# Three places of a two-block kernel: the first tiles, the head of the first feed-forward, and the last norm

## The chip, the cores and the metric

The kernel runs on one core of one Trainium2 chip. The metric is the device time of one execution in microseconds (us). Several executions of the kernel before were timed, and one more was profiled; times inside a profile count from the start of its span.

## The reference

Two transformer blocks follow each other on one sequence of 256 tokens with 1024 channels, in fp32. The first has a mixer of three parts (an RWKV-7 recurrence, a sparse attention, a state-space scan), a gated convolutional feed-forward of width 2816, and a gate by a second input. The second has a pooling layer and a dilated attention layer, each with its own feed-forward, and ends in a norm:

```python
def _rmsnorm(x, g):              # as rms_norm of the first block
    return x * lax.rsqrt(jnp.mean(x * x, axis=-1, keepdims=True) + eps) * g
...
h = _modulate(_rmsnorm(x, norm2_g[layer]), sh2, sc2)     # x_norm * (1 + sc2) + sh2
x = x + g2[:, None, :] * _conv_ffn(h, ffn_w_up[layer], ffn_conv_w[layer], ffn_conv_b[layer], ffn_w_down[layer])
...
return _rmsnorm(x, final_g)
```

The changed places compute: the first two tiles of `z = rms_norm(x, pre_mix_norm) @ w_in`; the start of `gelu(gate) * up`, where gate and up are the two halves of a causal depthwise convolution (three taps and a bias) of `x @ w_up`; the vectors `(1 + scale) * gain` of four later norms; and the last norm.

## The kernel before, in words

Activations lie transposed: channels on the 128 partitions in eight groups (`KT` = 8, index `k`), tokens along the free axis (`T` = 256). `h` is the residual. Each product is made in three passes of a reduced-precision fp32 format: an operand is split into a high part and a low part (the operand less its high part), and a tile sums high by high, high by low and low by high over the eight `k`, 24 products of 128x128 weights with 256 columns. A feed-forward's down tile sums over 22 channel groups, 66 products.

Weights are read in order through a ring of six slots of 1 MB (`ring`), issued by SP, which waits until the chunk six before is used. ScalarE writes a chunk's high part (`ring_hi`, four slots; `early_hi` for the first twelve chunks, which are those of the first projection), and GpSimd the low part in place (`ring_lo`); for the first twelve chunks VectorE does that, but GpSimd for the very first one (semaphore `first_lo`, L1483). On ScalarE the high parts stand between its other work: `reach(job)`, called before it reads the bank of `job`, makes all high parts whose slots depend on TensorE work older than that job; `take` calls it, `take0` does not. A second argument limits how many are made at a call.

TensorE opens a bank of PSUM for every job, in a rotation over eight banks; `opened` waits until the bank's previous job is given back by its reader. `close` counts finished jobs in `psum_ready`.

A norm: squares of `h` on ScalarE, six of them summed by VectorE, the sums over channels on TensorE against a column of 1/1024 (`mean_square_of`, job `("ms", i)`), square root on ScalarE (`root(i)`), reciprocal on VectorE into two columns of `rs` (tokens on the partitions, one column for each half of the tokens), and `spread(i)` on TensorE, which copies the two columns along all partitions by a product with the identity (job `("wd", i)`). VectorE then scales `h`.

The start: x is transposed in, normed with the squares taken over tokens' rows, and for each `k` VectorE scales, ScalarE writes the high part (`x_high`, 128x256 `hn_hi`), VectorE the low part (`x_split`, `hn_lo`). TensorE runs `first_tiles`: for each `k` two products with the high part of the activation (weights high and low) for both tiles, then all products with the low part. The parameter transposes (`("par", 0)`, `("par", 1)`) come behind them.

The first feed-forward (`ffn(0)`) works on pairs of tiles: gate ("ug") j and j+1, up ("uu") j and j+1. Its norm is divided out behind the product: for each tile VectorE multiplies by the spread root `wide_sb` (`normed`), ScalarE makes the last tap with the bias (`own`, into `ct`), VectorE adds the other two taps (`convolved`, 128x255 each), ScalarE takes GELU of the gate (`gated`), VectorE multiplies (`product`) and splits (`act_low`). The second tap of an up tile gives its bank back. VectorE's `second_gains` runs behind the first pair: four `(scale + 1) * gain` of 128x8 into `gsc`. They are used from the second block's first norm on, and GpSimd waits for them before it makes mask constants between its low parts.

The end: behind the last feed-forward's eight down tiles (`ffn(2)`), norm 9 runs as above, VectorE writes `h * final * wide` into `hn` for eight `k`, TensorE transposes sixteen 128x128 pieces into four banks (`("fin", n)`), VectorE copies two of them out and ScalarE two, and SP sends each half row block (128x512, 256 KB) to the output (L1440).

Line numbers: L549 is every product, L559 a transpose of `turn`, L1291 a transpose of attention, L2393 every ScalarE activation, L1646, L1653 and L1656 are VectorE's tensor-tensor, scalar-tensor-tensor and copy, L1579 a low part on GpSimd, L1483 that of the first chunk, L1531 and L1537 operations of GpSimd's sine tables.

## Time and profile before

| | us |
|---|---|
| runs of the kernel before | 1360.19, 1361.86, 1362.41 (median 1361.86) |
| the profiled execution | 1360.57 |
| its span | 1358.1 |
| TensorE busy in it | 1286.5 (95%) |
| VectorE, ScalarE, GpSimd busy | 571.7, 618.4, 845.2 |
| mean granted TensorE clock | 0.965 of full speed |

The span is the stretch between the first and the last instruction; the execution's own time is longer by what lies around it. Busy times of engines overlap each other. TensorE's products are pipelined: one may be listed as 0.28 us long while the next starts 0.12 us behind it.

### The profile page before, as it was taken

The page shows a single profiled execution, that of the slowest core. Times are in us where ns is not written, and L with a number is a line of the kernel's source. Part 1 is how long each engine was busy: PE and PEld are TensorE (multiplying, and loading weights), DVE is VectorE, ACT ScalarE, POOL GpSimd, SP SyncE. Part 2 cuts the span into 40 slices and gives each one's busy share as a digit, 9 for nine tenths or more (in the row PEclk, how much of TensorE's full clock was granted, in tenths as well). Part 3 has the DMA queues.
Part 4 walks back from the last instruction along what each step waited for, and adds up shares of the span by engine and source line. Part 5 has one row for each costly group of instructions (what it writes and reads, how often), then busy time and mean ns, then how long its engine had stood idle before and what let it go on. Part 6 is the DMA issues. An engine that isn't in the chain of part 4 may idle for free.

```text
span 1358.1 us, 25788 instructions
## 1 busy us (share of the span) xinstructions
PE 1286.5 (95%) x10741; PEld 1199.3 (88%) x10741; DVE 571.7 (42%) x1287; ACT 618.4 (46%) x953; POOL 845.2 (62%) x433
## 2 busy tenths in 40 slices
PE   6997989889899999898999999999999998999998
PEld 5983447779799999898999999999998888999997
DVE  5658676642676671522433303122222224433302
ACT  4540443125565554654544434554534454544431
POOL 7985400026689888555688776846655665888781
PEclk9998979989999999899999998999999999999998
DMA  8759985603455555425455555453648793455440
GB/s 265 199 168 361 328 293 189 216 31 113 136 187 186 175 176 182 152 94 187 141 180 180 167 193 165 140 156 93 188 127 256 240 294 122 155 179 182 165 162 31
DMA packets 232816, 242.81 MB, mean 179 GB/s; under 512 B 9068, under 2 KB 201726, under 8 KB 232702
## 3 DMA queue, kind: packets, MB, share of 16 engines
q1 hardware_dynamic: 232382, 241.08, 54.5%
q8 instruction: 85, 1.39, 0.4%
q14 instruction: 29, 0.24, 0.1%
q10 hardware_dynamic: 320, 0.10, 0.0%
HBM read 240.11 MB, written 1.05 MB: 178 GB/s over the span
## 4 chain that ended last, share of the span: by engine, by line
PE 90%; DVE 5%; ACT 2%; issue 2%; POOL 0%; ACTq 0%; DVEq 0%
PE banks L549 88%; DVE arena L1646 1%; PE banks L1291 1%; DVE arena L1653 1%; PE banks L559 1%; ACT ring_hi L2393 1%; ACT arena L2393 0%; DVE banks L1653 0%; DVE banks L1646 0%; POOL ring_lo L1483 0%; ACTq L1401 0%; PE banks L846 0%; ACT hn_hi L2393 0%; ACT hn L2393 0%; DVE hn L1653 0%
## 5 line engine op out<-in xcount | busy, mean ns | idle before, releaser
L1579 POOL TENSOR_TENSOR ring_lo<-ring,ring_hi 128x2048 fp32r<-128x2048 f32 (+1 forms) x176 | 718.8, 4095 | 437.0 <-ACT ring_hi L2393 436.8
L549 PE MATMUL banks<-hn_hi,ring_lo 128*128 128x256 f32 (+1 forms) x1864 | 528.8, 287 | 0.0
L549 PE MATMUL banks<-hn_hi,ring_hi 128*128 128x256 f32 x1696 | 484.0, 289 | 14.4 <-ACT hn_hi L2393 11.0
L549 PE MATMUL banks<-hn_lo,ring_hi 128*128 128x256 f32 x1696 | 446.4, 283 | 0.0
L2393 ACT ACTIVATE ring_hi<-ring 128x2048 fp32r<-128x2048 f32 (+1 forms) x176 | 299.6, 1705 | 172.1 <-PE banks L549 128.1
L549 PEld LDWEIGHTS banks<-hn_hi,ring_lo 128*128 128x128 f32 (+1 forms) x1864 | 366.0, 196 | 0.1
L549 PEld LDWEIGHTS banks<-hn_hi,ring_hi 128*128 128x128 f32 x1696 | 333.1, 196 | 18.0 <-issue 9.6
L549 PEld LDWEIGHTS banks<-hn_lo,ring_hi 128*128 128x128 f32 x1696 | 311.2, 192 | 0.1
L2393 ACT ACTIVATE arena<-banks 128x256 f32<-128x256 f32 (+6 forms) x240 | 94.0, 411 | 257.8 <-PE banks L549 176.4
L549 PEld LDWEIGHTS banks<-arena 64*128 64x128 f32 (+4 forms) x1282 | 118.9, 182 | 66.3 <-issue 42.6
L549 PE MATMUL banks<-arena 128*64 128x128 f32 (+9 forms) x1282 | 147.3, 309 | 24.4 <-DVE arena L1646 9.8
L549 PE MATMUL banks<-act_hi,ring_hi 128*128 128x256 f32 x528 | 149.6, 283 | 0.0
L549 PE MATMUL banks<-act_hi,ring_lo 128*128 128x256 f32 x528 | 149.4, 283 | 0.0
L549 PE MATMUL banks<-act_lo,ring_hi 128*128 128x256 f32 x528 | 149.4, 283 | 0.0
L1653 DVE SCALAR_TENSOR_TENSOR arena<-banks,par,arena 128x255 f32<-128x255 f32 (+1 forms) x187 | 89.6, 481 | 124.4 <-ACT arena L2393 122.0
L2393 ACT ACTIVATE arena<-banks,par 128x256 f32<-128x256 f32 x88 | 49.6, 564 | 122.6 <-PE banks L549 69.3
L549 PEld LDWEIGHTS banks<-act_lo,ring_hi 128*128 128x128 f32 x528 | 101.4, 192 | 0.0
L549 PEld LDWEIGHTS banks<-act_hi,ring_hi 128*128 128x128 f32 x528 | 101.4, 192 | 0.0
L549 PEld LDWEIGHTS banks<-act_hi,ring_lo 128*128 128x128 f32 x528 | 101.4, 192 | 0.0
L1653 DVE SCALAR_TENSOR_TENSOR h<-banks,mod,h 128x256 f32<-128x256 f32 x32 | 15.5, 484 | 133.7 <-PE banks L549 133.7
L2393 ACT ACTIVATE arena<-arena 128x256 f32<-128x256 f32 (+4 forms) x97 | 46.8, 511 | 39.7 <-DVE arena L1646 13.4
L549 PE MATMUL banks<-ring_lo,hn_hi 128*128 128x256 f32 x208 | 58.9, 283 | 0.0
(259 smaller groups left out, 1586.5 us busy)
## 6 DMA issues: line engine op xcount, KB each, us to landing
ring<-in_ada_w_dram SPq DMA_DIRECT2D x48, 1024.0 KB, 8.5
ring<-in_ffn_w_up_dram SPq DMA_DIRECT2D x44, 1024.0 KB, 5.2
ring<-in_w_up_dram SPq DMA_DIRECT2D x22, 1024.0 KB, 5.1
ring<-in_ffn_w_down_dram SPq DMA_DIRECT2D x16, 1024.0 KB, 5.0
ring<-in_w_kv_dram SPq DMA_DIRECT2D x15, 1024.0 KB, 5.4
ring<-in_w_in_dram SPq DMA_DIRECT2D x9, 1024.0 KB, 8.6
ring<-in_w_kv_dram SPq DMA_DIRECT2D x18, 512.0 KB, 3.8
ring<-in_attn_w_q_dram SPq DMA_DIRECT2D x18, 512.0 KB, 3.9
```

The lines of the kernel that those rows point to most:

```text
L549: return nc.tensor.matmul(o, l, r, start=start, stop=stop, **k)
L559: last = nc.tensor.transpose(b[0:m, off:off + n], src, ident[0:n, 0:n])
L1291: last = nc.tensor.transpose(b[:, br * P:br * P + P], dsc[s][:, x, k * P:k * P + P], ident[:, :])
L1579: led.emit(g.tensor_tensor(low, raw, high.bitcast(F32), ALU.subtract), sem("lo_ready"))
L1646: led.emit(v.tensor_tensor(o, x, y, op), signal, value)
L1653: led.emit(v.scalar_tensor_tensor(out=o, in0=x, scalar=s, in1=y, op0=op0, op1=op1), signal, value)
L2393: led.emit(nc.scalar.activation(o, x, func, **k), signal, value)
```

## The change

Four edits, made together. (a) The first two tiles: all products of high weights with the high activation, as each `k` comes, then high weights with the low activation, then low weights with the high activation; TensorE waits for the high part of the first chunk, and for GpSimd's low part only ahead of the last group. (b) At the first feed-forward, ScalarE makes one high part of weights ahead of `root(2)`, and behind the root a GELU of a constant column; the calls of `reach` in front of the first gate tile's own tap and in front of the first GELU are left out. (c) The four `second_gains` move from VectorE to GpSimd, as two operations each, ahead of the mask constants. (d) The last norm: ScalarE writes `h * final` (`h_last`, in the place of `hn_hi`) next to each square; TensorE transposes ten of its sixteen pieces between the second and third chunk of the last pair of down tiles, two more behind the squares' first sums, the last four behind the statistics. The root is not spread: VectorE (rows 0 to 127) and ScalarE (rows 128 to 255) multiply the transposed rows by its reciprocal, a column, as they copy them out.

```diff
@@ two_block_kernel
+        h_last = place("h_last", HN + KT * T, F32, KT, T)
@@ given_back
-                if i == 9:
-                    return sem("hn_ready"), KT
@@ chunk (TensorE)
                     if key == early[0]:
-                        pe.wait_ge(sem("first_lo"), 1)
+                        pe.wait_ge(sem("early_hi"), 1)
@@ TensorE, the start
-            first_tiles(-1, zt[:2], xz)
+            todo = []
+            for job, key, c0 in zt[:2]:
+                b = opened(job)[:, 0:T]
+                todo.append((b, [v[:, :, c0:c0 + P] for v in chunk(key)]))
+            for k in range(KT):
+                pe.wait_ge(sem("x_high"), k + 1)
+                for b, (_, w_hi) in todo:
+                    mm(b, w_hi[:, k, :], hn_hi[:, k, :], start=(k == 0), stop=False)
+            for k in range(KT):
+                pe.wait_ge(sem("x_split"), k + 1)
+                for b, (_, w_hi) in todo:
+                    mm(b, w_hi[:, k, :], hn_lo[:, k, :], start=False, stop=False)
+            pe.wait_ge(sem("first_lo"), 1)
+            for b, (w_lo, _) in todo:
+                for k in range(KT):
+                    last = mm(b, w_lo[:, k, :], hn_hi[:, k, :], start=False, stop=(k == KT - 1))
+                close(last)
@@ TensorE, ffn
+            def last_turn(s, k):
+                pe.wait_ge(sem("h_gained"), k + 1)
+                o = P * (k % 4)
+                return nc.tensor.transpose(last_banks[s, k // 4][:, o:o + P], h_last[:, k, s * P:s * P + P], ident[:, :])
+            last_banks = {}
...
+                        if f == 2 and (m, c) == (3, 1):
+                            current_job = current[0]
+                            for x in range(2):
+                                for s in range(2):
+                                    last_banks[s, x] = opened(("fin", s, x))
+                            current[0] = current_job
+                            for k in (0, 1, 2, 4, 5):
+                                for s in range(2):
+                                    last_turn(s, k)
...
-                mean_square_of(ms[0], b_ms, ms[1], (0, 6, 7))
-                spread(ms[0], f < 2)
+                if f < 2:
+                    mean_square_of(ms[0], b_ms, ms[1], (0, 6, 7))
+                    spread(ms[0])
+                else:
+                    mean_square_of(ms[0], b_ms, ms[1], (0, 6))
+                    for s in range(2):
+                        last_turn(s, 6)
+                    mean_square_of(ms[0], b_ms, ms[1], (7,))
+                    for k in (3, 7):
+                        for s in range(2):
+                            close(last_turn(s, k))
@@ TensorE, behind ffn(2, 9, (9, hn))
-            for s in range(2):
-                for f in range(2):
-                    for k in range(4):
-                        if s == 0:
-                            pe.wait_ge(sem("hn_ready"), 4 * f + k + 1)
-                    turn(("fin", 2 * s + f), [hn[:, 4 * f + k, s * P:s * P + P] for k in range(4)])
@@ SP
-                    sp.wait_ge(*freed(("fin", 2 * s + f)))
+                    sp.wait_ge(*freed(("fin", s, f)))
@@ GpSimd, behind low_parts(order[first_up:16])
-            pool.wait_ge(sem("gains"), 4)
+            pool.wait_ge(*freed(("adc", False)))
+            for n, (l, sc, gn) in enumerate(((0, 1, cols("norm1", 8)), (0, 4, cols("norm2", 8)), (2, 1, cols("kv_norm", 8)),
+                                             (1, 1, cols("norm1", 8, 8)))):
+                c0 = 48 * l + 8 * sc
+                led.emit(g.tensor_scalar(gsc[:, 8 * n:8 * n + 8], mod[:, c0:c0 + 8], 1.0, None, ALU.add))
+                led.settle()
+                led.emit(g.tensor_tensor(gsc[:, 8 * n:8 * n + 8], gsc[:, 8 * n:8 * n + 8], gn, ALU.mult), sem("gains"))
@@ VectorE, ffn (and second_gains itself)
                     if f == j == 0:
                         modulation_before(("uu", 0, 2))
-                        settle()
-                        second_gains()
...
+            dve.wait_ge(sem("gains"), 4)
             modulated(5, 0, 3, hn_lo, hn_hi, 0)
@@ VectorE, the end
-            wide, _ = norm_scale(9)
-            for k in range(KT):
-                stt(hn[:, k, :], h[:, k, :], col("final", k), wide, MUL, MUL, sem("hn_ready"))
-            for s in range(2):
-                b = take(("fin", 2 * s))
-                copy(outt[:, s, 0:512], b, *freed(("fin", 2 * s)))
+            placed(("ms", 9))
+            rec(rs_of(9)[:, 2:4], rs_of(9)[:, 0:2], sem("rs_small"))
+            settle()
+            for x in range(2):
+                b = take(("fin", 0, x))
+                ts(outt[:, 0, 512 * x:512 * x + 512], b, rs_of(9)[:, 2:3], MUL, signal=freed(("fin", 0, x))[0],
+                   value=freed(("fin", 0, x))[1])
@@ ScalarE, own and gated of ffn
                     if f == 0:
-                        reach((("ug", "uu")[x], f, j))
+                        if j or x:
+                            reach((("ug", "uu")[x], f, j))
...
                 def gated(j):
-                    reach(("uu", f, j))
+                    if f or j:
+                        reach(("uu", f, j))
@@ ScalarE, in front of ffn(0)
+            reach(("ms", 2), 1)
             root(2)
+            settle()
+            af(drv[:, 21:22], eps_col, ACT.Gelu_apprx_tanh)
             af(wide_sb, take0(("wd", 2))[:, 0:T], ACT.Identity, *freed(("wd", 2)))
@@ ScalarE, the end
-            summed_squares(9, hn, lambda k: gone(("down", 2, k), 99 if k < 7 else 0))
+            sqrt_table()
+            for k in range(KT):
+                gone(("down", 2, k), 99 if k < 7 else 0)
+                o = hn[:, k, :] if k else take0(("acc", 9))[:, 0:T]
+                af(o, h[:, k, :], ACT.Square, sem("squares"))
+                af(h_last[:, k, :], h[:, k, :], ACT.Identity, sem("h_gained"), scale=col("final", k))
             root(9)
-            for s in range(2):
-                b = take(("fin", 2 * s + 1))
-                af(outt[:, s, 512:1024], b, ACT.Identity, *freed(("fin", 2 * s + 1)))
+            act_.wait_ge(sem("rs_small"), NORM_ORDER.index(9) + 1)
+            for x in range(2):
+                b = take0(("fin", 1, x))
+                af(outt[:, 1, 512 * x:512 * x + 512], b, ACT.Identity, *freed(("fin", 1, x)), scale=rs_of(9)[:, 3:4])
```

## Rows read from the trace of the kernel before

**Rows 1.** The page, shares of the chain that ended last, by engine
```profile
PE 90%; DVE 5%; ACT 2%; issue 2%; POOL 0%; ACTq 0%; DVEq 0%
```

**Rows 2.** The chain in order of time, start: start us, us, what
```profile
12.24 4.52 POOL ring_lo L1483
16.85 8.07 PE banks L549 x48
```

**Rows 3.** Timeline, 0 to 50: start us, us, engine, line, operation, [idle before]
```profile
17.12 0.38 ACT L2393 ACTIVATE hn_hi<-banks 128x256 fp32r<-128x256 f32 x1 [0.47 <-DVE banks L1653]
...
21.25 0.41 PE L549 MATMUL banks<-hn_hi,early_hi 128*128 128x256 f32 x1
```

**Rows 4.** Timeline, 362.3 to 363.5: what releases TensorE
```profile
362.37 1.00 DVE L1653 SCALAR_TENSOR_TENSOR arena<-banks,par,arena 128x255 f32<-128x255 f32 x2 [2.65 <-ACT arena L2393]
363.43 0.58 PE L549 MATMUL banks<-hn_hi,ring_hi 128*128 128x256 f32 x1 [3.08 <-DVE arena L1653]
```

**Rows 5.** Timeline of ScalarE, 349 to 362
```profile
349.05 0.41 ACT L2393 ACTIVATE h<-banks 128x256 f32<-128x256 f32 x1
...
351.16 0.26 ACT L2393 ACTIVATE rs<-banks,drv 128x2 f32<-128x2 f32 x1 [1.70 <-PE banks L549]
353.74 0.38 ACT L2393 ACTIVATE arena<-banks 128x256 f32<-128x256 f32 x1 [2.32 <-PE banks L549]
...
355.82 0.56 ACT L2393 ACTIVATE arena<-banks,par 128x256 f32<-128x256 f32 x1
...
358.25 1.91 ACT L2393 ACTIVATE ring_hi<-ring 128x2048 fp32r<-128x2048 f32 x1
360.18 1.28 ACT L2393 ACT_TABLE_LOAD   x1
361.47 0.39 ACT L2393 ACTIVATE banks<-arena 128x256 f32<-128x256 f32 x1
```

**Rows 6.** The chain in order of time, 1343 to the end
```profile
1342.94 2.65 PE banks L549 x22
...
1347.25 0.27 ACT rs L2393
...
1347.95 0.70 PE banks L549 x4
...
1348.67 3.23 DVE hn L1653 x8
...
1354.98 0.60 ACT arena L2393
```

**Rows 7.** Timelines of VectorE at 367 and of GpSimd at 409
```profile
367.67 4.51 DVE L1653 SCALAR_TENSOR_TENSOR gsc<-mod,par 128x8 f32<-128x8 f32 x4 [0.33 <-DVE banks L1646]
...
409.29 18.53 POOL L1579 TENSOR_TENSOR ring_lo<-ring,ring_hi 128x2048 fp32r<-128x2048 f32 x4
```

**Rows 8.** Windows: length, PE busy (x), PEclk, DMA share, GB/s
```profile
345.00:350.00 5.00, 4.20 (x29) 1.00 0.00 0
360.00:365.00 5.00, 1.92 (x10) 0.79 0.40 140
364.00:543.00 179.00, 178.74 (x1484) 0.99 0.55 177
1356.00:1357.00 1.00, 0.00 (x0) 0.50 0.93 350
```

**Rows 9.** Timelines of GpSimd at 42 and 91, of VectorE at 92
```profile
42.27 2.26 POOL L1531 TENSOR_TENSOR arena<-arena 128x8 f32<-128x8 f32 x1
...
91.64 0.26 POOL L1537 MEMSET arena<- 128x192 f32 x1
...
92.10 2.48 DVE L1646 TENSOR_TENSOR arena<-banks,arena 128x512 f32<-128x512 f32 x4 [1.31 <-PE banks L549]
```

**Rows 10.** The chain in order of time: transposes of an attention step
```profile
1113.35 1.46 PE banks L1291 x12
```

**Rows 11.** Timeline of SP: the last output issue
```profile
1355.61 0.33 SPq L1440 DMA_DIRECT2D out_dram<-arena  x1
```

More of the change, by code:

```diff
@@ L2234, in _ @@
             rec(rs_of(2)[:, 2:4], rs_of(2)[:, 0:2], sem("rs_small"))
-            def second_gains():
-                for n, (l, sc, gn) in enumerate(((0, 1, cols("norm1", 8)), (0, 4, cols("norm2", 8)), (2, 1, cols("kv_norm", 8)),
-                                                 (1, 1, cols("norm1", 8, 8)))):
-                    c0 = 48 * l + 8 * sc
-                    stt(gsc[:, 8 * n:8 * n + 8], mod[:, c0:c0 + 8], 1.0, gn, ADD, MUL, sem("gains"))
             ffn(0)
```

## The prediction

> **What bounds the kernel now.** I read the shares of the chain of waits first: TensorE is on that chain for 90% of the span [rows 1]. So an edit pays only where TensorE stands idle, where its clock is low, or behind its last product. The list of TensorE's waits and the windows then say where that is. The diff touches three such places and one that only looks like one.
>
> The first is the start. The chain goes through GpSimd's low part of the first weight chunk (12.24 to 16.76) and then 48 products in 8.07 us [rows 2]. The reader should see that ScalarE makes the high parts of the activation meanwhile, one each 0.85 us (0.47 idle and 0.38 busy), the last until 17.50, and that 21.25 is the last product that takes 0.41: up to 21.5 they come 0.213 us apart (1.2 GHz), behind it 0.12 apart (2.4 GHz) [rows 3]. With 21 slow ones and 27 fast ones the 48 end at 24.7, and the row's 24.92 holds the last one's drain.
>
> The second is the head of the first feed-forward: TensorE idle for 3.08 us until 363.43, released by VectorE's second tap of the first "up" tile [rows 4], behind a chain on ScalarE [rows 5]. The third is the end, where from 1345.6 nothing but a serial chain is left [rows 6]. The place that only looks like one is VectorE's four gain products at 367.67, 4.51 us for 32 columns [rows 7]: from 364 to 543 TensorE is busy 178.74 of 179.00 us, 1484 products, 0.12 each [rows 8].
>
> **The start.** Removed: the wait of the first product for the low part. After: high-times-high products as ScalarE delivers, two every 0.85 us, the last pair at 17.53 to 17.95 (its part ends at 17.50 [rows 3]). Then 32 products that wait for nothing: VectorE's low parts of the activation run one step behind the high ones, and the weights' low part is there at 16.76 [rows 2]. If all 32 run at 0.213 us (1.2 GHz), they end at 17.95 + 6.8 = 24.8 against 24.7: nothing gained. If all run at 0.12, at 21.8: 2.9 us gained. The spaced pairs have no row at the low clock, so I do not know when it rises. I take the moment of before, 21.5: 16.7 products at 0.213 and 15.3 at 0.12 end at 23.3, a gain of **1.4 us**, since TensorE is now active earlier, if half idle. The Trainium skill ("TensorE: Matmul & The Clock Gate", Part 1) says that the moment at which the clock rises differs from run to run of one kernel; no run here shows it yet, and it would only spread this term.
>
> Does it carry? The parameter transposes follow the products, VectorE's copies follow them, and ScalarE's next weight chunk and the sine inputs follow those, so PE's stream to 90 us moves with them. The tight place is GpSimd's table chain, which ends at 91.90, while VectorE starts on it at 92.10 [rows 9]. It starts from ScalarE's sines and so moves too; but its operations are held when VectorE splits weights: one on 8 columns took 2.26 us [rows 9], while a fill of 192 columns takes 0.26. One such hold more eats 2 us and with it this term. Bounds -0.6 to 2.9.
>
> **The head of the feed-forward.** Chain before [rows 5]: root ends 351.42; copy of the spread root 353.74 to 354.12; then a high part of weights in front of the first own tap (355.82); another at 358.25, 1.91 us; then a table load of 1.28 at 360.18, the GELU at 361.47, and the own tap of "up" on which VectorE's taps (362.37, 1.00 for two) and TensorE wait [rows 4].
>
> After: one high part is moved to before the root. ScalarE's last copy of h ends at 349.46 and the root starts only at 351.16, when the statistics come [rows 5]; 349.5 + 1.9 = 351.4, so the root starts 0.25 later. It has slack: TensorE spreads it behind its first products, so that the copy of the spread comes at 353.74, 2.3 later. By the plan of chunks it is the one whose slots the output projection gave back before, so it waits for no TensorE work. The table load plus a dummy activation then take 351.7 to 353.2, and the copy at 353.74 stays. The own tap starts at 354.6, where VectorE's scaling of the tile (0.42 behind the copy) ends, not 355.8. VectorE's taps end at 356.2; second scaling 356.1 to 356.5; second own tap 356.6 to 357.1; GELU at 357.1 to 357.4. The second high part is not gone: the own tap of "up" still calls the loop that makes it, so it runs 357.4 to 359.3. Own tap of "up" 359.2 to 359.75, taps of VectorE to 360.8.
>
> TensorE runs dry at 360.35 as before (363.43 less 3.08, [rows 4]) and resumes at 360.8: 2.6 us earlier. Second, the clock. The window 360 to 365 has a granted clock of 0.79 with the 3 us gap in it, and the products from 363.43 to 366.15 come 0.21 apart; the window 345 to 350, where TensorE is idle for 0.80 us in several pieces, keeps 1.00 [rows 8]. So a gap of 0.45 keeps 2.4 GHz, and 14 products at 0.12 instead of 0.21 give 1.25 more. Together **3.9 us**. Lower bound: the gap stays as long as two high parts and a load take, 0.5; upper bound: no gap at all, 4.4.
>
> The Trainium skill ("ScalarE: Activation LUTs", What ACT_TABLE_LOAD costs) says that a switch of table costs 1.28 us of load and 1.38 us of drain, 2.66 in all. The trace agrees on the load and shows no drain: the high part before it ends at 360.16, the load starts at 360.18 and the GELU at 361.47 [rows 5]. By the page the preload would end at 354.3, 0.6 late for the copy, and this term would be 3.3.
>
> **The gains moved to GpSimd.** VectorE loses 4.51 us [rows 7] under cover of TensorE's full stream, so nothing is gained; if the cover were gone it would be worth 4.5. GpSimd gets eight operations on 8 columns, between its 16th low part and the mask constants. Unheld I put them at no more than the 0.26 of that fill, 2.1 us in all. Behind them in its queue are the low parts from 409.29 on [rows 7]. Counting tiles from 363.43 (24 products of 0.12, 2.88 us each, 18 tiles behind one that ends at 367.6), TensorE wants the first of those chunks at 419.4 and it is ready at 413.9 (a quarter of 18.53 us behind 409.29): 5.5 us of slack, and more once VectorE is not late. So 0, to a bound that is a rival below. SP's queue is not touched.
>
> **The end.** Removed [rows 6]: TensorE's spread of the root (0.70), eight scalings of h (3.23), sixteen transposes behind them, and the copies out in their old place. Added inside the down tiles: eight more ScalarE activations of 0.4, in idle time, since ScalarE waits for the tiles, and ten transposes behind the second chunk of the last pair. The h of tiles 0 to 5 is final by then and the four banks are those of tiles 2 to 5, both since the pair before. Twelve such transposes took 1.46 us elsewhere at the full clock [rows 10]: ten take **1.2 us**, wholly on TensorE's path.
>
> Behind the last product, in old times: last product 1345.59; statistics unchanged, since two transposes (0.24) fit ahead of the last square's arrival; root 1347.25 to 1347.52; reciprocal until 1347.82 (0.13 ahead of the spread at 1347.95); four transposes fit beside these. VectorE divides two half rows, 0.69 each, from 1347.9 to 1349.2; ScalarE two of 0.60 by 1349.2; a half row took it 0.60, and I take VectorE's as 0.1 slower. SP starts four transfers at 1348.65, 1349.3, 1349.65, 1350.0, where the last was issued at 1355.61 behind ScalarE's copy at 1354.98 [rows 6, 11], 2.5 us ahead of the span's end at 1358.1. Now the first would allow an end at 1348.65 + 2.5, but the other three queue for bandwidth behind it: 0.26 MB each at 350 GB/s [rows 8] is 0.75 us, so the end is 1348.65 + 2.5 + 2.25 = 1353.4. Gain 4.7, less 1.2: **3.5 us**. Bounds: 2.5 if ScalarE's and SP's steps slip a little, 4.5 if the transposes hide or transfers overlap.
>
> **Sum.** 1.4 + 3.9 + 0 + 3.5 = 8.8 us. The profiled execution took 1360.57 (span 1358.1), so it would become 1351.8; it lies 1.3 under the median 1361.86 of the runs shown. I forecast for the median: 1361.86 - 8.8 = **1353.1**.
>
> **Rivals.** (1) The gap at the first feed-forward stays, because the second high part is only moved one step and a bank or the clock still gives out. For it: the high part does remain between the GELU and the own tap. Against: the load and one high part are gone from the chain. Price 3.4: 1356.5. (2) The start gives nothing, because the clock rises late or GpSimd's tables get one more hold: 1354.5, and with (1) 1357.9. (3) The end gives little, because the division waits for transposes or ScalarE is late with h times its column: 2.5 less, 1355.6. (4) The change does not do what it says, every wait being taken up by the next: within 2.7 of before. For this speaks only that the three places are chains, and chains have a second-longest member. (5) Slower: GpSimd's eight small operations are each held as that one was, 2.26. That is 18.1 us [rows 9]; TensorE would stop for the next chunk once they take more than the 5.5 of slack, and the gain is used up at 5.5 + 8.8 = 14.3. At 18.1 the time is 1361.86 + 3.8 = 1365.7. Against it: VectorE's operations there read PSUM, and the hold that the rows show goes with a weight split at the start; but the gains themselves, 1.1 us a piece on VectorE [rows 7], show that these two engines hold each other here too.
>
> **How the numbers follow.** All three gains: 62%, own range 1350.8 to 1355.0. Rival 1: 12%. Rival 2 alone: 10%. Rival 3: 7%. (4): 5%. (5): 4%. Runs of one kernel spread by 1 us. Eight times in ten: 1350.6 to 1356.6, leaving out the last two and the tails. 0.2% (2.7 us) is about what a measurement of this kernel can tell from no change. Faster 0.91, same 0.05, slower 0.04.
>
> **What the profile will show.** First product near 12.5, transposes of parameters near 23.3, the low-clock stretch at the start no longer than before. ScalarE's table load near 351.7, TensorE's gap near 360.4 under 1 us and PEclk 1.00 in 360 to 370 less the shift. No gsc product on VectorE; eight on GpSimd near 404, each under 0.5. Ten transposes in the last down pair; from the end of the last product to the end of span 7.8 us where it was 12.5. It is wrong if the first gap only moves to the second pair of tiles, if the low clock outlives 24, or if transfers at the end take longer side by side.

## Result, and the profile after

| | kernel before | changed kernel |
|---|---|---|
| median of its runs, us | 1362.13 (6 runs, 1360.00 to 1363.76) | 1351.87 (6 runs, 1347.77 to 1353.43) |
| profiled execution, us | 1360.57 | 1351.78 |
| its span, us | 1358.1 | 1349.8 |
| TensorE busy, us | 1286.5 | 1284.6 |
| mean granted TensorE clock | 0.965 | 0.965 |

The ratio is 0.9932, with a 95% interval of 0.9911 to 0.9953: 9.3 us faster, 6.4 to 12.1. The medians of the table differ by 10.3, inside that interval; the spans of the two profiles differ by 8.3. The forecast was 8.8 less, 1353.1.

The shares of the chain hardly move against [rows 1], since 8 us are 0.6% of it. This is the page's part on the chain, by engine:

```profile
PE 89%; DVE 5%; ACT 2%; issue 2%; POOL 0%; ACTq 0%; DVEq 0%
```

**The start** answers to [rows 2, 3]. Timeline of TensorE in the changed kernel (start us, us, operation, count, idle before; L548 is every product there, L558 a parameter transpose):

```profile
12.56 0.96 PE L548 MATMUL banks<-hn_hi,early_hi 128*128 128x256 f32 x6 [1.67 <-ACT hn_hi L2426]
13.87 4.20 PE L548 MATMUL banks<-hn_hi,early_hi 128*128 128x256 f32 x10 [0.35 <-ACT hn_hi L2426]
17.86 3.19 PE L548 MATMUL banks<-hn_lo,early_hi 128*128 128x256 f32 x16
20.89 2.08 PE L548 MATMUL banks<-hn_hi,ring_lo 128*128 128x256 f32 x16
22.81 0.49 PE L558 MATMUL banks<-ident,arena 128*128 128x128 f32 x3
```

The first sixteen products take 5.3 us because they come with ScalarE's high parts; the next sixteen are still mostly 0.213 us apart, the last sixteen 0.12. The parameter transposes begin at 22.81; in the kernel before they did at 24.76, 1.95 later. What is said here of the clock at the start is read from the spacing of the products: the windows of the kernel before show a granted clock of 1.00 from 17 to 22 although its products come 0.213 us apart until 21.65, since its record of the clock begins only at 21.6. The changed kernel's record begins at 10.2 and has 0.50 from 13.6 to 20.4, as the spacing does.

**The head of the first feed-forward** answers to [rows 4, 5]. ScalarE (L2426 is each of its activations), then VectorE and TensorE at the gap, in the changed kernel:

```profile
348.12 1.95 ACT L2426 ACTIVATE ring_hi<-ring 128x2048 fp32r<-128x2048 f32 x1
349.97 0.26 ACT L2426 ACTIVATE rs<-banks,drv 128x2 f32<-128x2 f32 x1
350.45 1.28 ACT L2426 ACT_TABLE_LOAD   x1 [0.22 <-ACT rs L2426]
351.74 0.20 ACT L2426 ACTIVATE drv<-drv 128x1 f32<-128x1 f32 x1
352.55 0.39 ACT L2426 ACTIVATE arena<-banks 128x256 f32<-128x256 f32 x1 [0.60 <-PE banks L548]
...
356.18 1.90 ACT L2426 ACTIVATE ring_hi<-ring 128x2048 fp32r<-128x2048 f32 x1
357.98 0.55 ACT L2426 ACTIVATE arena<-banks,par 128x256 f32<-128x256 f32 x1
...
358.56 1.00 DVE L1693 SCALAR_TENSOR_TENSOR arena<-banks,par,arena 128x255 f32<-128x255 f32 x2 [1.22 <-ACT arena L2426]
...
359.62 0.38 PE L548 MATMUL banks<-hn_hi,ring_hi 128*128 128x256 f32 x1 [0.47 <-DVE arena L1693]
```

The high part of 1.95 us and the table load lie ahead of the copy of the spread root at 352.55; TensorE's gap is 0.47 us where it was 3.08. The windows of TensorE behind it (length, busy and products, granted clock, DMA share, GB/s) stay at the high clock, 19 or 20 products in 2 us, where [rows 8] had 0.79:

```profile
360.00:362.00 2.00, 2.00 (x20) 1.00 0.38 125
362.00:364.00 2.00, 2.00 (x19) 1.00 0.07 5
```

**The gains**, now on GpSimd (its timeline; L1635 adds, L1637 multiplies, L1613 is a low part):

```profile
399.09 0.25 POOL L1635 TENSOR_SCALAR gsc<-mod 128x8 f32<-128x8 f32 x1
399.49 0.21 POOL L1637 TENSOR_TENSOR gsc<-gsc,par 128x8 f32<-128x8 f32 x1
...
401.15 0.20 POOL L1637 TENSOR_TENSOR gsc<-gsc,par 128x8 f32<-128x8 f32 x1
...
403.23 4.64 POOL L1613 TENSOR_TENSOR ring_lo<-ring,ring_hi 128x2048 fp32r<-128x2048 f32 x1
```

Eight operations of 0.20 to 0.25 us end 2.26 us behind the start of the first; none is held. On VectorE four of them took 4.51 [rows 7].

**The end** answers to [rows 6]. The chain in order of time (L1161 is a last transpose, L1690 VectorE's division as it copies out), and SP's four issues:

```profile
1336.80 1.09 PE banks L1161 x10
1337.89 5.10 PE banks L548 x44
1343.00 0.28 PE banks L1161 x2
1343.27 0.58 PE banks L548 x4
...
1343.88 0.27 ACT rs L2426
...
1344.27 0.18 DVE rs L1699
...
1344.47 0.75 DVE arena L1690
...
1345.25 2.01 SPq L1474 DMA_DIRECT2D out_dram<-arena  x4
```

Ten transposes cost 1.09 us between the down tiles. The last down product ends at 1342.2 (the 5.10 us hold the first statistics too), and 7.6 us later the span ends; before it was 12.5, from 1345.6 to 1358.1. It is 12.5 in all four profiles with the old end and 7.6 in all seven with this one.

### The profile page after: what moved, and what is told of

It is laid out like the page before. It is cut to its first block, busy times and chain, and to the rows that moved or that the text cites. A ratio compares the mean times of both kernels' runs of the same rounds, so it can differ in the third digit from the quotient of the medians.

```text
span 1349.8 us, 25787 instructions
## 1 busy us (share of the span) xinstructions
PE 1284.6 (95%) x10737; PEld 1196.6 (89%) x10737; DVE 565.1 (42%) x1275; ACT 621.9 (46%) x962; POOL 849.4 (63%) x441
## 4 chain that ended last, share of the span: by engine, by line
PE 89%; DVE 5%; ACT 2%; issue 2%; POOL 0%; ACTq 0%; DVEq 0%
PE banks L548 87%; DVE arena L1686 2%; PE banks L1332 1%; DVE arena L1693 1%; DVE banks L1693 1%; PE banks L558 1%; ACT arena L2426 0%; DVE banks L1686 0%; ACT ring_hi L2426 0%; DVE arena L1897 0%; ACT hn_hi L2426 0%; ACTq L1435 0%; PE banks L861 0%; ACT hn L2426 0%; PE banks L984 0%
## 5 line engine op out<-in xcount | busy, mean ns | idle before, releaser
L1613 POOL TENSOR_TENSOR ring_lo<-ring,ring_hi 128x2048 fp32r<-128x2048 f32 (+1 forms) x176 | 719.0, 4098 | 431.1 <-ACT ring_hi L2426 430.8
L548 PE MATMUL banks<-hn_hi,ring_lo 128*128 128x256 f32 (+1 forms) x1864 | 524.7, 286 | 0.0
L548 PE MATMUL banks<-hn_hi,ring_hi 128*128 128x256 f32 x1696 | 483.5, 289 | 12.1 <-ACT hn_hi L2426 11.3
L548 PE MATMUL banks<-hn_lo,ring_hi 128*128 128x256 f32 x1696 | 446.5, 283 | 0.0
L2426 ACT ACTIVATE ring_hi<-ring 128x2048 fp32r<-128x2048 f32 (+1 forms) x176 | 299.7, 1705 | 170.7 <-PE banks L548 127.2
L548 PEld LDWEIGHTS banks<-hn_hi,ring_lo 128*128 128x128 f32 (+1 forms) x1864 | 363.0, 195 | 0.1
L548 PEld LDWEIGHTS banks<-hn_hi,ring_hi 128*128 128x128 f32 x1696 | 332.8, 196 | 15.6 <-issue 9.4
L548 PEld LDWEIGHTS banks<-hn_lo,ring_hi 128*128 128x128 f32 x1696 | 311.2, 192 | 0.1
L2426 ACT ACTIVATE arena<-banks 128x256 f32<-128x256 f32 (+6 forms) x238 | 92.8, 410 | 249.4 <-PE banks L548 173.9
L548 PEld LDWEIGHTS banks<-arena 64*128 64x128 f32 (+4 forms) x1282 | 119.3, 182 | 66.7 <-issue 43.0
L548 PE MATMUL banks<-arena 128*64 128x128 f32 (+9 forms) x1282 | 148.0, 309 | 24.6 <-DVE arena L1686 9.8
L548 PE MATMUL banks<-act_hi,ring_hi 128*128 128x256 f32 x528 | 149.7, 283 | 0.0
L548 PE MATMUL banks<-act_hi,ring_lo 128*128 128x256 f32 x528 | 149.4, 283 | 0.0
L548 PE MATMUL banks<-act_lo,ring_hi 128*128 128x256 f32 x528 | 149.4, 283 | 0.0
L2426 ACT ACTIVATE arena<-banks,par 128x256 f32<-128x256 f32 x88 | 49.8, 565 | 121.7 <-PE banks L548 69.6
L548 PEld LDWEIGHTS banks<-act_lo,ring_hi 128*128 128x128 f32 x528 | 101.4, 192 | 0.0
L548 PEld LDWEIGHTS banks<-act_hi,ring_lo 128*128 128x128 f32 x528 | 101.4, 192 | 0.0
L548 PEld LDWEIGHTS banks<-act_hi,ring_hi 128*128 128x128 f32 x528 | 101.4, 192 | 0.0
L2426 ACT ACTIVATE arena<-arena 128x256 f32<-128x256 f32 (+4 forms) x97 | 46.8, 512 | 39.9 <-DVE arena L1686 13.4
L548 PE MATMUL banks<-ring_lo,hn_hi 128*128 128x256 f32 x208 | 58.9, 283 | 0.0
```

Of the source, the lines that this page charges most:

```text
L548: return nc.tensor.matmul(o, l, r, start=start, stop=stop, **k)
L1613: led.emit(g.tensor_tensor(low, raw, high.bitcast(F32), ALU.subtract), sem("lo_ready"))
L2426: led.emit(nc.scalar.activation(o, x, func, **k), signal, value)
```

## Where the time went, place by place

I matched the instructions of the two traces and read how much earlier each comes, counted from the start of its span. Parameter transposes: 1.95. From 135, behind a wait of TensorE, to the first feed-forward 1.1 to 1.2. Behind its gap 3.8, and when the low clock of before is over (366) 5.1; 4.9 at 836. At 848 it is 6.3, and from 1141 on 4.5. The ten transposes take 1.1 (3.4 at the last product), the end gives 4.9: 8.3.

The steps at 848 and at 1141 have no edit near them. They are the granted clock behind two gaps of TensorE that both kernels have. First the kernel before, then the changed one (windows of TensorE):

```profile
842.00:844.00 2.00, 2.00 (x12) 0.50 0.00 0
844.00:846.00 2.00, 2.00 (x11) 0.50 0.00 0
846.00:848.00 2.00, 2.00 (x13) 0.59 0.01 4
...
1138.00:1140.00 2.00, 0.87 (x7) 1.00 0.00 0
1140.00:1142.00 2.00, 2.00 (x19) 1.00 0.09 9
```

```profile
838.00:840.00 2.00, 2.00 (x12) 0.60 0.00 0
840.00:842.00 2.00, 2.00 (x19) 1.00 0.00 0
...
1134.00:1136.00 2.00, 2.00 (x11) 0.50 0.00 0
1136.00:1138.00 2.00, 2.00 (x17) 0.86 0.25 58
```

Behind the gaps from 838.6 to 841.5 (833.7 to 836.6 in the changed kernel) TensorE made 27 products at 0.21 us before and 12 after: 15 fewer at 0.093 more than the 0.12 of the high clock, 1.4 us won. Behind the gap at 1137 (1131) the kernel before kept 2.4 GHz and the changed one fell to 1.2 GHz for 14 products more; with a gap 0.3 longer that is most of the 1.8 lost. A second profile of the changed kernel has both steps again (+1.4 and -1.8). But that does not make them a part of the change, nor of where its work lies in time, as the profiles of the experiments below show. At the first place 26 or 27 slow products follow in six of the thirteen profiles (the kernel before, the four edits alone, the gains put back) and 12 or so in the other seven; the gap ends at 838.2 and 839.3 in two of the six and at 839.8 in one of the seven. At the second place the clock also falls in the kernel with edit (d) alone, which gets there 1.6 later than the kernel before and has no edit ahead of it; it does not fall in two variants of the changed kernel that get there about as early as that one does. So these steps belong to no edit, and what decides them stays open.

## Experiments

First the four edits alone, in the same rounds. In each, only the named part of the diff ahead of the prediction is made.

**(a) alone.**

```diff
-            first_tiles(-1, zt[:2], xz)
+            for k in range(KT):
+                pe.wait_ge(sem("x_high"), k + 1)
+                for b, (_, w_hi) in todo:
+                    mm(b, w_hi[:, k, :], hn_hi[:, k, :], start=(k == 0), stop=False)
...
```

> Only the reordered first two tiles; all else as before. My account of the changed kernel: the parameter transposes come 2.0 us earlier, of which some is lost again by 135, because the clock goes up and down at other moments. So transposes near 22.8 (24.76 before), and the head of the first feed-forward 1 to 2 us earlier; whole 1359.5 to 1361. Rival, GpSimd's tables keep the time of before: the 2 us are gone by 92 and the whole is 1361.9. Second rival, the order of the products makes no difference to the clock: then the low clock ends at 21.5 as before and the transposes come at 23.4.

Measured: 1360.99 (10 runs) against 1361.12 (31 runs), ratio 0.9995, 0.9976 to 1.0015. The timeline of TensorE:

```profile
18.07 3.62 PE L549 MATMUL banks<-hn_lo,early_hi 128*128 128x256 f32 x16
21.48 2.63 PE L549 MATMUL banks<-hn_hi,ring_lo 128*128 128x256 f32 x16
23.95 0.49 PE L559 MATMUL banks<-ident,arena 128*128 128x128 f32 x3
```

Here the second group runs wholly at the low clock and the third partly: the transposes begin 0.8 ahead of before's. Over all profiles with this start the new order begins them at 22.81, 22.89, 23.16, 23.32, 23.47, 23.64 and 23.95, the old one at 24.76, 25.07, 25.13 and 25.28; the means are 1.74 us apart. The clock rises at 20.4 to 22.75 in the one and at 21.65 to 22.5 in the other, in kernels that are alike up to there. By the Trainium skill ("TensorE: Matmul & The Clock Gate", Part 1) that moment differs from run to run of one kernel; these rows agree. TensorE's matched products are 0.9 ahead of the kernel before from 30 to 98, 0.2 at 118, 0.4 late at 128 and 0.8 late at 135. Two places take it. The first is the tight place that the prediction named: VectorE's operations at 92 wait here for GpSimd's last table operation and not for TensorE, and are 0.2 ahead where VectorE was 0.9 ahead at 90. The second is the clock. Around 130 TensorE stands idle, 3.2 us before and 2.7 here, and takes up work near 133.2 in both; the low clock lasts from about 134.2 to 141.1 before and from about 132 to 142.2 here. So in this profile the start's gain was made and then lost, and more than it.

**(b) alone.**

```diff
+            reach(("ms", 2), 1)
             root(2)
+            settle()
+            af(drv[:, 21:22], eps_col, ACT.Gelu_apprx_tanh)
```

(and the two calls of `reach` left out, as in the change)

> Only the edits of ScalarE's queue at the first feed-forward. Theory: TensorE's gap there is 0.4 to 0.6 us instead of 3.08, no low clock behind it, 3.8 us earlier from there on; whole 1358.0. VectorE still has its four gains of 4.5 us behind the first pair, now 4 us nearer to TensorE. Rival, which speaks for edit (c): the bank of the second gate tile then comes late and TensorE waits 1 to 3 us near 370, so that only 1 to 3 us stay. Rival from the page on tables (a switch costs 2.66 us): the copy of the spread root is 0.6 us late and the gain is 3.2.

Measured: 1357.86 against 1361.12, ratio 0.9979, 0.9960 to 0.9999. Matched products go from 0.8 late ahead of the gap to 3.1 early behind it, 3.9 won; then 0.8 is given back at 374 to a second wait of TensorE (0.6 us), for a bank that VectorE holds. That wait is the next experiments' matter.

**(c) alone.**

```diff
-                        settle()
-                        second_gains()
+                led.emit(g.tensor_scalar(gsc[:, 8 * n:8 * n + 8], mod[:, c0:c0 + 8], 1.0, None, ALU.add))
+                led.settle()
+                led.emit(g.tensor_tensor(gsc[:, 8 * n:8 * n + 8], gsc[:, 8 * n:8 * n + 8], gn, ALU.mult), sem("gains"))
```

> Only the gains moved to GpSimd. Theory: 0; TensorE's gap stays 3.08 and it has no wait from 364 to 543; VectorE's first act_low of the second tile comes 4.5 us earlier with nobody waiting for it. The whole is within 1 us of before. Rival: low parts on GpSimd become late by its eight operations (2.2 us) and TensorE waits: up to 2 us slower. Second rival: the 4.5 us on VectorE mattered and the whole gains 1 us or more.

Measured: 1360.76 against 1361.12, ratio 1.0002, 0.9983 to 1.0022. VectorE's matched instructions are 4.2 us early at 372 and level again by 425; TensorE's wait at the head stays 3.1. Nothing, as forecast, for the edit alone.

**(d) alone.**

```diff
-                mean_square_of(ms[0], b_ms, ms[1], (0, 6, 7))
-                spread(ms[0], f < 2)
...
+                            for k in (0, 1, 2, 4, 5):
+                                for s in range(2):
+                                    last_turn(s, k)
...
```

> Only the last norm. Theory: nothing moves before the last pair of down tiles; ten transposes take 1.1 us there, from the end of the last product to the end of the span it takes 7.6 us instead of 12.5: 3.8 us in all, 1358.0. Rival, the eight added ScalarE activations delay the weights' high parts in the down tiles: TensorE then has a wait before the last pair and the gain is under 3. Second rival, transfers at the end are slower side by side: 8.5 us or more behind the last product.

Measured: 1354.06 against 1361.12, ratio 0.9953, 0.9933 to 0.9972: 6.4 us, with 3.8 at the interval's near end. In its profile the transposes cost 1.1 and the end gives 4.9, so 3.8 is what the place shows; the other 2.6 of the 6.4 have no place in the trace. That profile is of the longest of its ten runs (1360.62, span 1358.3): at 1160, ahead of anything edited, it is 4.1 us behind the kernel before, 2.5 of them lost from 1140 on, where its clock is low twice. The four ratios sum to 0.7 + 2.9 - 0.3 + 6.4 = 9.7 us, the change gave 9.3. With some 2.7 us to either side of each, this says no more than that they may add.

Then four variants of the changed kernel, one run each, beside a run of the kernel before of 1362.84. What they show is read from their traces; one run says little of the time.

**The own tap of the first up tile no longer makes a high part.**

```diff
-                        if j or x:
+                        if j:
                             reach((("ug", "uu")[x], f, j))
```

> The changed kernel, and the second high part of weights is moved one step further back, behind the first up tile's own tap. Theory: the gap of 0.47 us near 359 closes, since VectorE's taps end 1.3 us earlier; 0.4 to 0.5 us earlier from there on, and no new wait, since GpSimd's low part of that chunk has over 3 us of slack. Rival: the chunk's low part is late and TensorE waits later on for it, nothing gained or a loss of 1 us.

Measured: 1351.77, span 1349.9. TensorE has no wait left between 350 and 380, and its matched products are 0.57 us further ahead behind the place than ahead of it. So the remaining 0.47 was the second high part, as the prediction's chain had it; one run cannot show the half microsecond in the total.

**The low products of the activation between the high ones.**

```diff
+                for k0 in ([k - 1] if k else []) + ([k] if k == KT - 1 else []):
+                    pe.wait_ge(sem("x_split"), k0 + 1)
+                    for b, (_, w_hi) in todo:
+                        mm(b, w_hi[:, k0, :], hn_lo[:, k0, :], start=False, stop=False)
```

(in the first loop over `k`; the second loop is gone)

> The changed kernel, and at the start the two products with the low part of step k-1 stand behind the two with the high part of step k, instead of in a pass of their own. TensorE is then busy from 12.6 on, and 18 products instead of 32 are left at 17.9. Theory that the clock rises with how busy TensorE was: it rises near 17.5 and the parameter transposes come near 20.3 instead of 22.8. Rival, it rises at the same moment (20.8 in the changed kernel's profile): transposes near 21.5. Either way 1.2 to 2.5 us earlier there; whether it carries to the end depends on GpSimd's tables (ready 0.2 us ahead of use before): if they bind, 0 to 1 us is left behind 92.

Measured: 1350.32, span 1348.5. Its TensorE:

```profile
18.24 2.08 PE L548 MATMUL banks<-hn_hi,ring_lo 128*128 128x256 f32 x16
20.16 0.49 PE L558 MATMUL banks<-ident,arena 128*128 128x128 f32 x3
```

With TensorE busy all the way the clock rises at 15.7, and the transposes begin at 20.16, 2.65 ahead of the changed kernel. 1.7 of it is left at 60 and 1.3 from 800 on; the spans differ by 1.3. Here too VectorE waits at 92 for GpSimd's tables, and 1.0 goes there.

**Without the preload of the table.**

```diff
-            settle()
-            af(drv[:, 21:22], eps_col, ACT.Gelu_apprx_tanh)
```

> The changed kernel without the GELU of a constant that brings the table in early. The load then stands in front of the first real GELU. Theory from the rows (1.28 us, no drain): ScalarE's own tap of the first up tile is 1.28 later and TensorE's gap there is 0.47 + 1.28 = 1.75 us. The page on tables gives 2.66 a switch: gap of 3.1 us, and a low clock behind it. Either way nothing changes ahead of 355.

Measured: 1354.90, span 1353.1. The load (1.28 us) stands in front of the GELU again; TensorE's timeline and windows:

```profile
361.02 0.39 PE L548 MATMUL banks<-hn_hi,ring_hi 128*128 128x256 f32 x1 [1.89 <-DVE arena L1693]
...
362.00:364.00 2.00, 2.00 (x11) 0.50 0.00 0
```

The gap grows by 1.42, to 1.89; of the two values expected, 1.75 is the near one and 3.1 is not. Behind it the products come 0.21 apart until about 365. Matched products are level ahead of the gap, 1.4 late behind it and 2.9 once the clock is back: 2.9 us in all for one preload, half of them clock.

**The gains back on VectorE.**

```diff
+                        settle()
+                        second_gains()
```

(and GpSimd's eight operations out again)

> The changed kernel with the four gains back on VectorE behind the first pair. Theory, by the plan of banks: the second gate tile's bank is given back at 368.3 instead of 363.8 and TensorE wants it at 359.6 + 3 x 2.88 = 368.3: it waits 0 to 0.5 us, so the move of the gains is worth next to nothing even here. Rival: it is worth 1 us or more in this place, because VectorE, ScalarE and GpSimd all run late behind it.

Measured: 1356.12, span 1354.2. The timelines of GpSimd and VectorE, and TensorE's waits (us in all, times, longest):

```profile
364.52 4.61 POOL L1613 TENSOR_TENSOR ring_lo<-ring,ring_hi 128x2048 fp32r<-128x2048 f32 x1 [0.74 <-ACT ring_hi L2428]
...
364.87 4.28 DVE L1687 SCALAR_TENSOR_TENSOR gsc<-mod,par 128x8 f32<-128x8 f32 x1 [0.34 <-DVE banks L1680]
...
369.08 0.31 DVE L1687 SCALAR_TENSOR_TENSOR gsc<-mod,par 128x8 f32<-128x8 f32 x3
...
PE banks L548 <- DVE act_lo L1680: 0.6, 1, 0.6
PE banks L548 <- DVE arena L1687: 0.5, 1, 0.5
```

The bank that VectorE holds while it makes the gains is wanted 0.6 us sooner than it is free: matched products go from 1.0 late to 1.85 late at 369, 0.8 us, as in (b) alone. The 4.51 us of [rows 7] are not four slow operations. The first takes 4.28 and ends at 369.15, 0.02 behind GpSimd's low part of 4.61; the other three take 0.15 each. It is the same in the kernel before (4.28 to 371.95, the low part to 371.93) and in (b) alone. Another 2.5 us are lost later, in steps such as 1.1 by 890 and 0.9 near 1056, where nothing differs from the changed kernel.

Last, a variant of the end, and it together with two of those above, timed in the same rounds as the changed kernel once more.

**All sixteen transposes behind the statistics.**

```diff
-                            for k in (0, 1, 2, 4, 5):
-                                for s in range(2):
-                                    last_turn(s, k)
...
+                            for k in range(4 * x, 4 * x + 4):
+                                last = last_turn(s, k)
+                            close(last)
```

> The changed kernel with all sixteen last transposes behind the statistics; none stands between the down tiles. My theory, that the ten inside are wholly on TensorE's path (1.1 us by the changed kernel's trace) while the six behind the statistics hide beside root and reciprocal: the last product ends 1.1 us earlier, eight transposes of the first two banks take 1.0 us from the statistics on, where root and reciprocal take 1.2 to 1.5 us, so the first two divisions start as early behind it as now; the second two wait 0.3 us at most. The sending is bound by the bandwidth of four transfers, so from the last product to the end of the span stays 7.6 to 7.9 us: 0.8 to 1.1 us faster than the changed kernel, about 1351.0 by its median 1351.9. Rival, that the sixteen stand in the way of the divisions: the first division starts 1 us later behind the last product, and the time equals the changed kernel's. Against the kernel before, 0.9925 by the first and 0.9932 by the second.

Measured: 1352.26, ratio to the kernel before 0.9944, 0.9922 to 0.9967; the changed kernel in these rounds 1352.57. The chain in order of time:

```profile
1342.83 0.61 PE banks L548 x4
1343.44 1.82 PE banks L1161 x16
...
1345.28 0.69 ACT arena L2422
```

The last product comes 1.1 us earlier against the matched products before the transposes. From VectorE's last addition to its first division it is 2.23 us, as in the changed kernel (2.22), and from SP's first issue to the span's end 4.65 (4.55), though ScalarE's second half row now waits. So 1.0 us is won at the place, as the first theory said. The medians, 0.3 apart with runs that spread over 2 us and more, cannot show it, and this profile stood 0.7 behind that of the changed kernel before it reached the end.

**All three together, and the changed kernel again.**

```diff
+                for k0 in ([k - 1] if k else []) + ([k] if k == KT - 1 else []):
...
+                            for k in range(4 * x, 4 * x + 4):
...
-                        if j or x:
+                        if j:
```

> The changed kernel with three more edits: one call fewer that makes a high part (in front of the first up tile's own tap), the low products of the activation set between the high ones of the first two tiles, and all sixteen last transposes behind the statistics. My theory, that the three add, since TensorE's own stream is the bound between the places: 0.5 (the gap at the first feed-forward gone), 2.0 (the start, which a look at it alone kept until 1340) and 1.0 (transposes off the path) is 3.5 us less than the changed kernel: 1348.4, ratio to the kernel before 0.990. Rival, that the start's part is eaten up at GpSimd's tables or by stretches of low clock, as it was when edit (a) was made alone: 1.5 less than the changed kernel, 1350.4, ratio 0.9915.

> The changed kernel itself on the same chip and in the same rounds, so that the other two can be set against it: 0.9932 of the kernel before, as measured first, 0.9911 to 0.9953.

Measured: 1349.54 (1346.84 to 1352.54), ratio 0.9925, 0.9903 to 0.9947, against 1352.57 (1348.27 to 1353.88), ratio 0.9939, 0.9916 to 0.9962, of the changed kernel. By medians it is 3.0 us faster than the changed kernel, by the ratios 1.9; the intervals overlap, so that it beats the kernel before is shown and that it beats the change is likely only. The theory asked for 3.5 less than the changed kernel, the rival for 1.5. Its profile says where the rest went: the first feed-forward and the end keep their 0.6 and 1.0, but at the start the transposes of the parameters begin at 20.54, 2.3 ahead of the changed kernel, and the clock falls behind the idle time there (products from 24.9 on 0.21 apart, where the mixed start alone had 0.12); at 57 nothing is left of the 2.3. The second profile of the changed kernel has a span of 1351.2, 1.4 longer than the first, all of it lost before 135.

## Why the prediction was right

**The start, 1.4.** The order of events was right: first product at 12.56 (forecast near 12.5), parameter transposes at 22.81 (23.3), on average of seven profiles 23.3. The clock rose at 21.3 on average, where the forecast took 21.5. The gain at the place is 1.74 on average. Whether it carries is another matter. Seven profiles have this start and four the old one, with nothing else changed up to 340: on average the seven are 1.8 ahead of the four at 60, 1.4 at 120 and 1.0 at 340. Single ones differ much: ahead of the feed-forward the result's profile is 1.2 early against that of the kernel before, the second profile of the same changed kernel 0.25 late, that of (a) alone 1.1 late. So the 1.2 of the result's profile is near 1.4 partly by luck. The prediction named GpSimd's tables as the tight place, and it was right: in five of the seven VectorE waits at 92 for GpSimd's last table operation, 1.75 to 2.0 us, and gives up 0.4 to 0.7. VectorE's timeline, first the changed kernel's, then that of its second profile:

```profile
90.11 2.48 DVE L1686 TENSOR_TENSOR arena<-banks,arena 128x512 f32<-128x512 f32 x4 [1.31 <-PE banks L548]
```

```profile
91.62 2.48 DVE L1686 TENSOR_TENSOR arena<-banks,arena 128x512 f32<-128x512 f32 x4 [2.01 <-POOL arena L1571]
```

What it did not have is the second loss, to the low clock around 130 to 142. The time of (a) alone cannot tell 0 from 1.4. This is the term that the runs leave least sure.

**The head, 3.9.** Right in each link. With the 1.2 us that the stream was early, the forecast had the table load at 350.5, the resumption at 359.6 and a gap of 0.45; it was 350.45, 359.62 and 0.47. The shift grew from 1.2 to 5.1, which is 3.9. It grows by 3.9 in each of the six profiles with this head unaltered, and by under 0.05 in the three of the edits (a), (c) and (d) alone. That a gap of 0.45 keeps 2.4 GHz and is worth 1.25 more is borne out: the shift grows by 1.3 from 363.4 to 366, where the kernel before has its slow products, and in the kernel without the preload those behind 1.89 us of gap cost 1.5. The second high part stayed in the chain, as said; leaving it out closed the gap. The load was followed by its first activation 0.01 us behind it here too, without the drain that the Trainium skill ("ScalarE: Activation LUTs", What ACT_TABLE_LOAD costs) adds.

**The gains, 0.** Right for the edit alone and wrong inside the change, by 0.8 us. The step that failed is "VectorE loses 4.51 us under cover of TensorE's full stream": the cover was read from the kernel before, where TensorE came 3 us late to that stretch. With (b) made, it comes earlier by as much, and 0.6 us of the 4.51 sticks out. The prediction also read the 4.51 as 1.1 us a piece; it is one operation that ends with a low part of GpSimd, and three of 0.15. That GpSimd's operations would each be held 2.26 was rival 5; they took 0.20 to 0.25.

**The end, 3.5.** Measured 4.9 less 1.1, 3.8. From the last product to the end 7.6 against 7.8 forecast; ten transposes 1.09 against 1.2; from the first issue to the end 4.55 against 4.75, which was reckoned with the four transfers one behind the other.

**Sum.** 1.2 + 3.9 + 0 + 3.8 = 8.9, less 0.6 for the two stretches of clock (+1.4 and -1.8) and smaller steps, is the 8.3 of the spans. (The gains' 0.8 is not a part of it: it is what the head would have lost.) The interval of the ratio, 6.4 to 12.1, holds it. Steps of 1 to 2 us that no term of the forecast has cancelled in this profile; in the second one, 6.9 shorter than the kernel before, they did so again, but the start's term was gone. Of the rivals, (1), (3), (4) and (5) are excluded by the profile. (2) is not: the place moved as forecast, but its second cause, GpSimd's tables, was at work in five of seven profiles, and in two of seven ahead of the feed-forward nothing of the start was left against the kernel before.

## What to carry to other kernels

Read cover from the kernel as it will be: an edit priced at nothing because its neighbour is late is worth something once the neighbour is on time. When a few small operations show a long time, look at each: here one of four waited out a long operation of another engine. When a gap on TensorE is shortened, price the clock behind it with the gap, here a third of the head's 3.9 and half of the preload's 2.9. And give a gain at the start of a long stream less trust than one at its end: every later gap at which the clock may fall can take or give a microsecond, while the tail behind the last product keeps what it wins.

## What the hardware showed beside this

- The clock behind one and the same gap differs between profiles: 26 or 27 slow products behind the gap at 838 in six of them, 12 or so in seven; and behind an idle time of 2.18 us near 1137 it fell in four profiles and did not in four. The first changed with the shift of the stream in all but one profile, the second did not go by it. Each is worth 1.3 to 1.8 us.
- In the unchanged start of four kernels the clock rose at 21.65, 22.31, 22.50 and 22.53. With TensorE half idle from 12.6 on it rose at 20.4 to 22.75 (seven profiles); with it busy nearly all the time from 12.6 on, at 15.7 and 17.1 (two).
- A VectorE operation of 128x8 that starts 0.35 us behind a low part of GpSimd (128x2048, 4.61 us) takes 4.28 us and ends with it, in three profiles; the next three of its kind take 0.15 each. Eight operations of the same width on GpSimd, between its own low parts, take 0.20 to 0.25 each. It also goes the other way: GpSimd's 2.26 us on 128x8 at 42.27 [rows 9] end at 44.53, VectorE's weight split of 2.28 us at 44.47. No run moved one of the two operations alone.
